# Two attention score products that contract over the 64 partitions of their head, without zero-padded key buffers

## What is computed

```python
logit_own = (jnp.einsum('hqd,hkd->hqk', qc, k_own).astype(jnp.float32) * scale
             - slopes[:, None, None] * dist_own)              # first block, 8 heads of 64
...
p_s = masked_softmax(jnp.einsum('bghqd,bgqkd->bghqk', qb, k_sel), ...)   # second block, selected keys
p_w = masked_softmax(jnp.einsum('bghqd,bgkd->bghqk', qb, k_w), m_w)      # second block, window keys
```

## Time and profile before

| | |
|---|---|
| time, median of 3 runs (lowest, highest) | 1343.54 us (1341.25, 1349.25) |
| the profiled execution's own time | 1340.13 us |
| its span in the profile | 1338.1 us |
| TensorE matmuls busy | 1246.7 us (93%) in 6326 instructions |
| VectorE busy | 642.6 us (48%) |
| ScalarE busy | 317.1 us (24%) |
| GpSimd busy | 580.2 us (43%) |
| mean granted clock of TensorE | 0.969 |
| score matmuls (L449) | two recorded matmuls for each of 96 scores |

### The profile page before, as it was taken

How to read it: one execution, slowest core, us unless ns; L and a number is a source line. 1 busy time by engine, 2 the same in 40 slices (tenths; PEclk the granted TensorE clock), 3 DMA queues, 4 the chain that set the end, 5 groups by cost and what they waited for, 6 DMA issues and landing times.

```text
span 1338.1 us, 17644 instructions
## 1 busy us (share of the span) xinstructions
PE 1246.7 (93%) x6326; PEld 1034.9 (77%) x6326; DVE 642.6 (48%) x1189; ACT 317.1 (24%) x639; POOL 580.2 (43%) x332
## 2 busy tenths in 40 slices
PE   7898899998799799999997999998999999999996
PEld 6676688887688677788786888876888888888885
DVE  3974546548472478563735444457153500153202
ACT  3114221121472123311213344431031200021001
POOL 5543323322104456454420333334666666666662
PEclk9998999999899899999977999999999999999998
DMA  6211111100101222223420111112223232222321
GB/s 234 95 63 47 48 33 47 47 32 31 48 1 48 86 78 95 64 79 111 150 79 17 48 48 48 48 51 77 82 92 97 98 104 94 95 94 94 115 89 63
DMA packets 28870, 99.29 MB, mean 74 GB/s; under 512 B 3472, under 2 KB 5904, under 8 KB 28176
## 3 DMA queue, kind: packets, MB, share of 16 engines
q1 hardware_dynamic: 26592, 91.60, 20.7%
q10 hardware_dynamic: 2224, 6.94, 1.5%
HBM read 95.39 MB, written 2.10 MB: 73 GB/s over the span
## 4 chain that ended last, share of the span: by engine, by line
PE 55%; DVE 3%; issue 1%; ACT 0%; DVEq 0%; ACTq 0%
PE acc L266 15%; PE acc L268 15%; PE acc L267 15%; PE aux L449 3%; PE aux L467 2%; PE aux L716 2%; PE aux L457 1%; PE aux L745 0%; PE aux L641 0%; PE aux L328 0%; DVE mt_lo L1238 0%; DVE merged_b L1246 0%; PE aux L761 0%; DVE k_padded L1125 0%; DVE normalized L1288 0%
## 5 line engine op out<-in xcount | busy, mean ns | idle before, releaser
L1338 POOL CAST w_hi<-w_raw 128x1024 fp32r<-128x1024 f32 x164 | 175.0, 1067 | 724.7 <-issue 530.3
L1340 POOL TENSOR_TENSOR w_lo<-w_raw,w_hi 128x1024 fp32r<-128x1024 f32 x164 | 405.0, 2470 | 13.2
L266 PE MATMUL acc<-ht_hi,w_hi 128*128 128x512 f32 x672 | 283.5, 422 | 9.3 <-DVE feature_major L1588 5.1
L268 PE MATMUL acc<-ht_hi,w_lo 128*128 128x512 f32 x672 | 265.6, 395 | 0.0
L267 PE MATMUL acc<-ht_lo,w_hi 128*128 128x512 f32 x672 | 265.1, 394 | 0.0
L266 PEld LDWEIGHTS acc<-ht_hi,w_hi 128*128 128x128 f32 x672 | 128.9, 192 | 40.7 <-issue 8.9
L267 PEld LDWEIGHTS acc<-ht_lo,w_hi 128*128 128x128 f32 x672 | 128.9, 192 | 30.3 <-issue 4.3
L268 PEld LDWEIGHTS acc<-ht_hi,w_lo 128*128 128x128 f32 x672 | 128.0, 190 | 28.0
L266 PE MATMUL acc<-w_hi,ht_hi 128*128 128x512 f32 x256 | 106.4, 416 | 0.3 <-DVE feature_major L1009 0.3
L268 PE MATMUL acc<-w_hi,ht_lo 128*128 128x512 f32 x256 | 101.3, 396 | 0.0
L267 PE MATMUL acc<-w_lo,ht_hi 128*128 128x512 f32 x256 | 101.0, 395 | 0.0
(11 more groups left out here) (350 smaller groups left out, 1950.5 us busy)
## 6 DMA issues: line engine op xcount, KB each, us to landing
w_raw<-units SPq DMA_DIRECT2D x164, 512.0 KB, 3.3
cmp_w<-w_kv ACTq DMA_DIRECT2D x4, 1024.0 KB, 5.2
residual<-x SPq DMA_DIRECT2D x4, 512.0 KB, 6.9
result<-normalized SPq DMA_DIRECT2D x4, 512.0 KB, 2.8
consts_sb<-consts SPq DMA_DIRECT2D x1, 1344.5 KB, 11.4
norm_post_sb<-norm_post ACTq DMA_DIRECT2D x1, 512.0 KB, 4.7
cmp_tokens<-feature_major ACTq DMA_DIRECT2D x4, 128.0 KB, 2.9
final_sb<-final_g ACTq DMA_DIRECT2D x1, 512.0 KB, 3.3
```

What stands on the lines that cost most here:

```text
L266: nc.tensor.matmul(bank, ah, bh, start=start, stop=False)
L268: return nc.tensor.matmul(bank, al, bh, start=False, stop=stop)
L1338: nc.gpsimd.tensor_copy(w_hi[:, slot], raw[:, j]).then_inc(hi_split, 1)
L1340: nc.gpsimd.tensor_tensor(w_lo[:, slot], raw[:, j], w_hi[:, slot].bitcast(F32), ALU.subtract).then_inc(w_split, 1)
```

## The change

The scores take only the 64 partitions of their head from the staged queries and from the keys. So the keys need no zeros beside them. In the first block the scaled keys go into a buffer `keys1` of four chunks, filled by one multiply of 128x512 for each chunk; in the second the scores read PB2 directly. The memsets and the half-height multiplies and copies are gone. The semaphore k_padded is renamed. `ya_hi` moves from 120 KB to 160 KB, since its old place overlaps the key chunks of PB2 (122 to 126 KB), which are now read to the end of the attention.

```diff
--- before.py
+++ after.py
@@ -202,7 +202,7 @@
 
         G["MA0"], G["MA1"], G["XS"], G["WN"] = G["TG"], G["IB"], G["EG"], G["DEC"]
 
-        kz = sb("k_padded", [P, 4, 2, T], F32, 96)
+        keys1 = sb("keys_scaled", [P, 4, T], F32, 96)
         q_st1 = sb("q_staged", [P, 2, T], F32, 192)
         pr1 = sb("probs", [P, 4, T], F32, 180)
         pt1 = sb("probs_t", [P, 2, T], F32, 188)
@@ -446,8 +446,9 @@
                 if n >= B.ring:
                     pe.wait_ge(biased, first + n - B.ring + 1)
                 w = (t + 1) * P
-                nc.tensor.matmul(B.scores[n % B.ring][:, :w], B.q_st[:, n // 8 % 2, t * P:(t + 1) * P],
-                                 keys(n)[:, :w], start=True, stop=True).then_inc(scored, 1)
+                rows = slice(n // NT % 2 * DH, n // NT % 2 * DH + DH)
+                nc.tensor.matmul(B.scores[n % B.ring][:, :w], B.q_st[rows, n // 8 % 2, t * P:(t + 1) * P],
+                                 keys(n)[rows, :w], start=True, stop=True).then_inc(scored, 1)
 
             def flip(n):
                 pe.wait_ge(probs, first + n + 1)
@@ -542,7 +543,7 @@
 
         post_in = sem("post_in")
         names = ("x_squares normalized ba_split ba_product ba_row_out ba_flipped ba_tanh ba_in ba_exps "
-                 "sp_log conv_done conv_silu k_padded g_flip g_copy g_square g_reduced gate_sums "
+                 "sp_log conv_done conv_silu keys_ready g_flip g_copy g_square g_reduced gate_sums "
                  "gate_cols gate_exps gate_done tg_ready row_sums qk_ready e_ready dec_in dec_ready u0 "
                  "t0 t0_out masked merged x_ready x_out tx_ready solved wt_ready wn_out vn_ready vn_out "
                  "o_ready o_out o_square z_silu mixed_squares post_done go_done ").split()
@@ -584,7 +585,6 @@
         rope_t = sb("rope_temp", [P, 2, T], F32, 194)
         pos = sb("positions_sb", [P, T], I32, 202)
 
-        kz2 = sb("k_padded_2", [P, 2, 2, T], F32, 160)
         kc2 = sb("cmp_tokens", [P, 2, 2, T], F32, 198)
         xc = sb("cmp_blocks", [P, 2, 2, 8, 2, CMP_C], F32, 176)
         w1 = sb("cmp_w1", [P, 2, 8, 256], F32, 96)
@@ -605,7 +605,7 @@
 
         gate_a = sb("gate_tanh_a", [P, 8, T], F32, 96)
         gate_b = sb("gate_tanh_b", [P, 8, T], F32, 180)
-        ya_hi, ya_lo = sb("ya_hi", [P, 4, T], F32R, 120), sb("ya_lo", [P, 4, T], F32R, 196)
+        ya_hi, ya_lo = sb("ya_hi", [P, 4, T], F32R, 160), sb("ya_lo", [P, 4, T], F32R, 196)
         yb_hi, yb_lo = sb("yb_hi", [P, 4, T], F32R, 112), sb("yb_lo", [P, 4, T], F32R, 160)
         mt_hi, mt_lo = sb("mt_hi", [P, KD, T], F32R, 128), sb("mt_lo", [P, KD, T], F32R, 144)
         TM = sb("merged_b", [P, 2, T], F32, 168)
@@ -777,7 +777,7 @@
                 a = n // STEPS * P + n // NT % 2 * DH
                 return VSW[:, j, a:a + DH]
 
-            attention_on_tensor(pe, SELECTED, 2 * STEPS, branch_banks, lambda n: kz2[:, n // STEPS, n // NT % 2],
+            attention_on_tensor(pe, SELECTED, 2 * STEPS, branch_banks, lambda n: PB2[:, 13 + n // STEPS],
                                 branch_values, branch_fill)
             pe.wait_ge(values_used, WINDOW + STEPS + 1)
             flip_on_tensor(pe, lambda t, k: YB[:, t, k * P:(k + 1) * P], 4, FLIP_B)
@@ -1117,12 +1117,6 @@
             eng.wait_ge(on["h_summed"], HG + 1)
             step(V.tensor_scalar(h_ss, h_ss, 1.0 / DG, EPS, ALU.mult, ALU.add))
             rsqrt(step, h_ss, h_rs, t32[:, 0:16])
-
-            step(V.memset(kz2[:], 0.0))
-            for s in range(2):
-                for g in range(2):
-                    rows = slice(g * DH, (g + 1) * DH)
-                    step(V.tensor_copy(kz2[rows, s, g], PB2[rows, 13 + s]))
 
             eng.wait_ge(pe_in, 16)
             eng.wait_ge(on["cmp_moved"], 16 * 8)
@@ -1452,10 +1446,10 @@
                     fill = slab_in_pieces(pe, n * UPS + U_Q1, ht_hi, ht_lo, n + SLAB_Q1, by_token)
                     delta_tile_on_tensor(pe, n, fill)
 
-            pe.wait_ge(on["k_padded"], 1)
+            pe.wait_ge(on["keys_ready"], 1)
             for b in range(4):
                 pe.wait_ge(acc_out[b], SLAB_O1)
-            attention_on_tensor(pe, MOBA, STEPS, moba_banks, lambda n: kz[:, n // 8, n // NT % 2],
+            attention_on_tensor(pe, MOBA, STEPS, moba_banks, lambda n: keys1[:, n // 8],
                                 lambda n, j: V1[:, j, n // NT * DH:(n // NT + 1) * DH], lambda n: None)
 
             pe.wait_ge(on["go_done"], NT)
@@ -1700,13 +1694,10 @@
                 eng.wait_ge(on["o_square"], n + 1)
                 step(V.tensor_reduce(go_ss[:, four], G["AT"][:], AX, ALU.add))
 
-            def pad_keys(m):
+            def scale_keys(m):
 
                 if m < 4:
-                    step(V.memset(kz[:, m], 0.0))
-                    for h in range(2):
-                        rows = slice(h * DH, (h + 1) * DH)
-                        step(V.tensor_tensor(kz[rows, m, h], PB[rows, 16 + m], R[rows], ALU.mult))
+                    step(V.tensor_tensor(keys1[:, m], PB[:, 16 + m], R[:], ALU.mult))
 
             for n in step.loop(NT - 1, 15):
                 delta_tile_on_vector(n, lambda m: None, lambda n: prepare_tile(n + 1), False)
@@ -1716,12 +1707,12 @@
             def make_alibi(n):
 
                 step(V.tensor_copy(alibi[0][:], const("alibi")))
-                V.tensor_scalar(alibi[1][:], const("alibi"), 0.5, None, ALU.mult).then_inc(on["k_padded"], 1)
-
-            delta_tile_on_vector(NT - 1, pad_keys, make_alibi, True)
+                V.tensor_scalar(alibi[1][:], const("alibi"), 0.5, None, ALU.mult).then_inc(on["keys_ready"], 1)
+
+            delta_tile_on_vector(NT - 1, scale_keys, make_alibi, True)
             step(V.tensor_scalar(go_ss, go_ss, 1.0 / DG, EPS, ALU.mult, ALU.add))
             rsqrt(step, go_ss, go_rs, t32[:, 0:16])
-            eng.wait_ge(on["k_padded"], 1)
+            eng.wait_ge(on["keys_ready"], 1)
             eng.wait_ge(on["z_silu"], 1)
 
             def beside(n):
```

## The result

| | before | after |
|---|---|---|
| time, median (lowest, highest) | 1342.39 us (1338.27, 1349.25), 4 runs | 1394.19 us (1390.63, 1394.46), 4 runs |
| ratio to before, 95% interval | | 1.037 (1.033 to 1.041) |
| profiled span | 1338.1 us | 1391.5 us |
| mean granted clock of TensorE | 0.969 | 0.943 |

A forecast was written before the change was run, and what follows sets the result against it. TensorE was taken to bound the kernel. Score pauses of +31.6 us, less 5.3 and 11.4 us for the dropped key fillings, gave +14.9 us on the 1343.54 us median: 1358.4 us, range 1325 to 1372.

The forecast's parts named there:

- What bounds the kernel: Whole kernel: TensorE, busy 1246.7 of 1338.1 us; a change pays only where it shortens TensorE's streams or waits.
- The pause of a 64-row score: Both attentions: changing shape into and out of each score costs 0.13 + 0.21 = 0.34 us, 93 times, +31.6 us.
- The hand-over of products half as wide in columns: Half-width products at L661 to L663, used to price a score's pauses: 0.19 going in, 0.21 coming out.
- rival 1: Scores of both attentions: no pause, only the VectorE gains count, 1327 us; chance 0.27.
- The two fills: Key filling dropped in the first block's last delta-rule tile, -5.3 us, and ahead of the second block's compression, -11.4 us.
- Tile: Last delta-rule tile, L1678 to L1692: 21.7 us without the first block's key filling, 27.09 before.
- compression: Start of the second block's compression products: no TensorE wait, full clock, 2.9 + 5.9 + 2.6 = 11.4 us saved.
- rival 2: Compression products: pauses as forecast, but the clock falls there all the same, 1367 us; chance 0.10.
- The sum: Whole kernel: pauses 31.6, less fills 5.3 and 11.4, = +14.9 us, giving 1358.4 us.
- Rival 3: First attention: pauses and half-empty array take the clock down, about 44 us more, 1402 us; chance 0.05.
- nothing but the drops behind idle times: All the prediction cited for a clock fall in the first attention: clock drops seen after TensorE's idle times.
- 0.99 there before: First attention: granted clock of 0.99 in the kernel before, cited against the clock falling there.

The follow-up runs named there:

- e4: Kernel before, with every product of the first attention's steps on rows 0 to 63, half of each sum left out, flips as ordinary products; 1400.02 us, ratio 1.040.
- e8: Kernel before, with the first attention's flips as ordinary products with the identity, all on 128 rows, nothing left out; 1350.20 us, ratio 1.003.
- e3: Kernel before, plus a small extra product of 128 rows and 64 columns ahead of every first-attention score, bringing pauses without 64-row products; 1358.60 us, ratio 1.009.
- e5: Changed kernel, plus 24 extra full products in TensorE's wait ahead of the first score, so the first attention begins at full clock; 1397.55 us, ratio 1.038.
- e6: Changed kernel, with the zeros moved to the staged queries, keys unpadded and scores contracting 128 partitions again; 1332.73 us, ratio 0.988 to the kernel before.

## Why the prediction missed

**What bounds the kernel: right.** TensorE set the pace in both attentions.

**The pause of a 64-row score: right.** 0.34 us forecast, 0.34 measured in the second attention, 0.22 of it on the way out. The hand-over of products half as wide in columns was the right stand-in for products half as high; rival 1 (no pause) was wrong. At half clock the pause hardly grows, by this estimate: if the rest of a step takes twice as long, it is (12.20 - 2 x 5.49) / 4 = 0.31 us; e4's four steps fell 0.44 us short of twice e8's, and with that it is 0.41.

**The two fills: right.** Tile 21.64 for 21.7; compression 11.3 for 11.4, and the clock did not fall there, so rival 2 was wrong.

**What failed: the clock of the first attention.** The sum priced the scores of that stage at their pauses alone, 0.34 us each, and left what a lower clock costs there at nothing; it cost 36.7 us. Rival 3 named the place, both ingredients and the size (1402 us, 44 us more than the forecast). The stage grew by 46.9; 30 x 0.34 = 10.2 of it are the pauses, which leaves 36.7 for the clock. The rival had a chance of 0.05, the range stopped short of it, and for it stood "nothing but the drops behind idle times". Two steps led there. The first: I took the busy share and "0.99 there before" as evidence for the clock after the change. It was evidence only for products on all rows; after, TensorE is busy for 60.00 of 60.00 us at 0.50. The Trainium skill (TensorE: Matmul & The Clock Gate, Part 1: The HAM clock gate) also has the clock follow how busy TensorE has been; the trace differs if busy means having a product in flight, and e4 against e8 shows that the rows in use count. The second: I costed the scores of both attentions in one line of the sum. They have the same price of a pause, but a score of the first has only transposes and values beside it, and one of the second six full weight products more. What dilutes a disturbance should have been read for each stage. "Pauses and half-empty array" was also one ingredient too many: e3 shows that the pauses alone leave the clock at 1.00.

**The sum** with the clock in it: 14.9 + 36.7 = 51.6 us, against 49.5 (44.6 to 54.5) measured. The 36.7 are read from the result, so this shows only that no other term is missing.

## What to carry over

In this kernel a contraction over fewer partitions saved TensorE nothing and put its clock at risk: if such products make up much of a stage, fill the other rows at the same time with a second product of the same width (two heads side by side), or pad the smaller operand with zeros once. When a change alters how much of the array a product uses, give a fall of the clock its own look for each stage: what else streams between these products, and on how many rows. A busy share of 100% with half the instruction count is how it shows.

## What was not expected of the hardware

- A TensorE that is never idle can sit at 1.2 GHz: 80 us in e4 with 20.00 of 20.00 us busy in each stretch of 20, and from a full-clock start in e5.
- Useless work can pay for itself: six full-row fillers per score add 192 products, and the time stays about where it was (1398 for 1394).
- Two fp32 products on the two halves of the rows, issued back to back into different banks, run side by side in full: 1.13 us for both, 1.12 for one.
- Rows that hold zeros count as filled: 128-row scores with zeros on 64 of the rows keep the full clock, with the zeros in the keys (before, 0.99) or in the queries (e6, 1.00), and 64-row scores do not (0.50).
- The two pauses of a score take 0.34 us at the full clock and, by an estimate, 0.31 to 0.41 at the lower one; they don't double.
- Between one and six fillers it is a matter of chance: with three, executions of one and the same kernel lay between 1396 and 1443 us. Where the border lies was not tried further.
